# Sample attention in four 32-column groups of TensorE, old-key transposes in two parts, three unread products in the final stage

## What is computed

```python
def sample_attention(q, k_new, v_new, k_cache, v_cache, rel_bias):
    k = jnp.concatenate([k_cache, k_new], axis=1)      # 512 old rows + 16 new ones
    v = jnp.concatenate([v_cache, v_new], axis=1)
    ...
    return band_attention(q, k, v, q_pos, k_pos, k_pos >= 0, rel_bias)

def band_attention(q, k, v, q_pos, k_pos, k_valid, rel_bias):
    s = jnp.einsum('nqhd,nkhd->nhqk', q, k) * (HEAD_DIM ** -0.5)
    ...                                                # + bias by clipped distance
    p = jax.nn.softmax(s, axis=-1)
    return jnp.einsum('nhqk,nkhd->nqhd', p, v)
```

## Time and profile before

| | us |
|---|---|
| median of three runs | 1889.56 (1889.5 to 1892.87) |
| profiled execution, its own time | 1889.39 |
| profiled execution, span | 1887.7 |
| sample attention, from the first key transpose to the first product of the convolution | 455.26 to 570.61 |
| one steady turn of its loop | 13.33 |
| final stage, from the last expert's result to the end | 1830.4 to 1887.7 |

### The profile page before, as it was taken

The page is one execution under the profiler, slowest core; times in us unless marked ns, Lnnn a source line. Parts: engine busy times, 40 slices in busy tenths (PEclk is TensorE's granted clock), DMA queues, the critical chain, the costliest instruction groups (busy, mean ns, idle before and its releaser), DMA issues.

```text
span 1887.7 us, 22614 instructions
## 1 busy us (share of the span) xinstructions
PE 1708.9 (91%) x8539; PEld 1399.3 (74%) x8539; DVE 947.6 (50%) x1156; ACT 755.3 (40%) x869; POOL 261.1 (14%) x327
## 2 busy tenths in 40 slices
PE   6984999999989999999999997189999999999976
PEld 1244987887549989999999786177777777877753
DVE  0451101554321263222213544858888888888857
ACT  0221123664111112111112222157777777777753
POOL 2003501110000000000000000402121212212003
PEclk9996999999999999999999998589999999999988
DMA  9757622002512110121114433089999999999967
GB/s 343 279 99 204 207 73 73 1 1 92 160 68 79 36 45 27 51 83 52 47 51 136 181 124 134 15 330 397 400 396 400 397 399 398 398 399 397 400 223 276
DMA packets 194749, 371.36 MB, mean 197 GB/s; under 512 B 10700, under 2 KB 69108, under 8 KB 194547
## 3 DMA queue, kind: packets, MB, share of 16 engines
q1 hardware_dynamic: 170784, 289.92, 42.7%
q0 software_dynamic: 18976, 62.93, 10.4%
q10 hardware_dynamic: 4914, 17.49, 2.3%
HBM read 324.49 MB, written 47.89 MB: 197 GB/s over the span
## 4 chain that ended last, share of the span: by engine, by line
PE 72%; DMA 12%; DVE 8%; issue 3%; ACT 2%; another core or an unknown queue 2%; SPq 0%; POOL 0%; DVEq 0%; ACTq 0%; PEldq 0%; POOLq 0%
PE ps L1547 12%; PE ps L1548 12%; PE ps L1549 12%; DMA mraw<-in_w_e_down_dram 9%; PE ps L1530 4%; PE ps L1870 4%; PE ps L1871 4%; PE ps L1877 3%; PE ps L1674 3%; PE ps L1655 2%; PE ps L1897 2%; PE ps L1905 2%; PE ps L1898 2%; PE ps L1737 2%
## 5 line engine op out<-in xcount | busy, mean ns | idle before, releaser
L1064 DVE TENSOR_TENSOR mlo<-mraw,mhi 128x2048 fp32r<-128x2048 f32 x188 | 427.5, 2289 | 78.0 <-ACT mhi L931 77.8
L931 ACT CAST mhi<-mraw 128x2048 fp32r<-128x2048 f32 x192 | 366.6, 1913 | 111.5 <-DMA mraw<-in_w_e_down_dram 76.4
L1547 PE MATMUL ps<-hTh,ring_r 128*128 128x384 f32 x864 | 291.3, 337 | 38.3 <-DVE ring_r L1064 31.1
L1548 PE MATMUL ps<-hTl,ring_r 128*128 128x384 f32 x864 | 290.5, 336 | 0.0
L1549 PE MATMUL ps<-hTh,ring_r 128*128 128x384 f32 x864 | 290.2, 336 | 0.0
L1870 PE MATMUL ps<-mhi,xTh 128*128 128x512 f32 x512 | 204.6, 400 | 2.7 <-DVE xTl L1064 2.4
L1871 PE MATMUL ps<-mhi,xTl 128*128 128x512 f32 x512 | 201.5, 394 | 0.0
L1547 PEld LDWEIGHTS ps<-hTh,ring_r 128*128 128x128 f32 x864 | 163.5, 189 | 39.7 <-DVE ring_r L1064 29.3
L1064 DVE TENSOR_TENSOR ring_r<-ring_f,ring_r 128x1024 fp32r<-128x1024 f32 x56 | 68.3, 1224 | 197.8 <-ACT ring_r L741 197.4
L1548 PEld LDWEIGHTS ps<-hTl,ring_r 128*128 128x128 f32 x864 | 163.6, 189 | 0.0
L1549 PEld LDWEIGHTS ps<-hTh,ring_r 128*128 128x128 f32 x864 | 163.6, 189 | 0.0
(11 more groups left out here) (304 smaller groups left out, 2604.7 us busy)
## 6 DMA issues: line engine op xcount, KB each, us to landing
mraw<-in_w_e_gate_dram SPq DMA_DIRECT2D x64, 1024.0 KB
mraw<-in_w_e_up_dram SPq DMA_DIRECT2D x64, 1024.0 KB
mraw<-in_w_e_down_dram SPq DMA_DIRECT2D x64, 1024.0 KB, 12.6
aring<-in_w_ada_dram SPq DMA_DIRECT2D x24, 1024.0 KB
ring_f<-in_w_in_dram SPq DMA_DIRECT2D x80, 256.0 KB, 4.5
y_d<-yy ACTq DMA_DIRECT2D x32, 512.0 KB, 6.8
y_d<-zrow POOLq DMA_DIRECT2D x68, 128.0 KB, 4.1
kc<-in_cache_attn_k_dram SPq DMA_DIRECT2D x8, 1024.0 KB, 5.9
```

The costliest lines, as they stand in the source:

```text
L931: nc.scalar.copy(mhi[j][:], mraw[j][:]).then_inc(s["gu_hi" if j < 4 else "d_hi"], 1)
L1064: V.tensor_tensor(out, value, high.bitcast(F32), ALU.subtract).then_inc(sig, 1)
L1547: mm(out, xh, wh, start=start, stop=False)
L1548: mm(out, xh, wl, start=False, stop=False)
```

## The change

Scores: `qblk` now holds 32 columns for each head pair, without the zeros. Each head pair's product has a 32-column weight and writes its own 32 partitions of the bank; nothing is added up over the four. In the built program these products carry a tile of 128 rows by 32 columns at column 0, 32, 64 or 96. Values: for every head pair, a 32-column piece of `PTs` is multiplied with that pair's 128 columns of `vc`, again into its own 32 partitions, so 16 + 4 products of 128 columns take the place of 4 + 1 of 512, and the result is 128x128. `atts` becomes 128x128, its transpose one product into bank 7, and `sample_cols` two copies of 64x4x16. PE's wait for `ks_at` moves from ahead of the transposes of `Ps` to ahead of the values. The old-key transposes are cut into two halves, with the second behind the transposes of `Ps`; `k_tr` counts to two for a sequence, and ACT's copy needs only the first half. In the final stage PE waits for all 18 `wdiag` and runs three products into bank 7 that nobody reads.

```diff
-        qblk = at("qblk", [P, 2, 640], X(9))
+        qblk = at("qblk", [P, 2, HP, 32], X(9))
...
             def old_keys(q):
-                wait(sp, s["k_tr"], q - 1)
+                wait(sp, s["k_tr"], 2 * (q - 1))
...
             def old_keys_half(q):
-                act.wait_ge(s["k_tr"], q + 1)
+                act.wait_ge(s["k_tr"], 2 * q + 1)
...
             def old_keys_rest(q):
-                dve.wait_ge(s["k_tr"], q + 1)
+                dve.wait_ge(s["k_tr"], 2 * q + 2)
...
             def sample_cols(q):
                 dve.wait_ge(s["ks_att"], q + 1)
-                for h in range(H):
-                    m, rows = h // 2, slice(HD * (h % 2), HD * (h % 2) + HD)
-                    c = m * P + h * DEC
-                    V.tensor_copy(qT[rows, m, NP_TOK + q * DEC:NP_TOK + (q + 1) * DEC], ps[rows, 6, c:c + DEC]
+                cols_of = ps[:, 7, P:2 * P].rearrange("p (m h t) -> p m h t", m=HP, h=2)
+                for h_ in range(2):
+                    rows = slice(HD * h_, HD * h_ + HD)
+                    V.tensor_copy(qT[rows, :, NP_TOK + q * DEC:NP_TOK + (q + 1) * DEC], cols_of[rows, :, h_, :]
                                   ).then_inc(s["ks_at"], 1)
...
                 for m in range(HP):
-                    mm(ps[:, 4, :], qb[:, m, :], kcT[:, m, :], start=(m == 0), stop=(m == HP - 1))
+                    mm(ps[32 * m:32 * m + 32, 4, :], qblk[:, q % 2, m, :], kcT[:, m, :], start=True, stop=True)
...
                 if q + 1 < SEQS:
-                    old_keys_t(q + 1)
+                    old_keys_t(q + 1, 0)
                 pe.wait_ge(s["ks_p"], q + 1)
                 wait(pe, s["ks_ptc"], 2 * q)
-                wait(pe, s["ks_at"], H * q)
...
+                if q + 1 < SEQS:
+                    old_keys_t(q + 1, 1)
                 pe.wait_ge(s["ks_ptc"], 2 * q + 2)
                 wait(pe, s["ks_ev"], q)
+                wait(pe, s["ks_at"], 2 * q)
...
                 for c in range(4):
-                    mm(ps[:, 7, :], PTs[:, c, :], vc[:, r, c, :], start=(c == 0), stop=False)
-                mm(ps[:, 7, :], PTs[0:DEC, 4, :], v16[:, r, :], start=False, stop=True).then_inc(s["ks_pv"], 1)
+                    for m in range(HP):
+                        mm(ps[32 * m:32 * m + 32, 7, 0:P], PTs[:, c, 32 * m:32 * m + 32],
+                           vc[:, r, c, m * P:(m + 1) * P], start=(c == 0), stop=False)
+                for m in range(HP):
+                    last = mm(ps[32 * m:32 * m + 32, 7, 0:P], PTs[0:DEC, 4, 32 * m:32 * m + 32],
+                              v16[:, r, m * P:(m + 1) * P], start=False, stop=True)
...
+            pe.wait_ge(s["f_w"], 2 * NT)
+            for j in range(3):
+                mm(ps[:, 7, :], wdiag[:, 0, j, :], wdiag[:, 0, 4:8, :], start=True, stop=True)
             for t in range(NT):
-                pe.wait_ge(s["f_w"], 2 * t + 2)
```

More of the change, by code:

```diff
@@ L205, in build @@
         Ss = at("Ss", [P, NK], X(0))
-        atts = at("atts", [P, DA], X(3))
+        atts = at("atts", [P, P], X(3))
         v16 = at("v16", [DEC, 2, DA], X(5))
-        qblk = at("qblk", [P, 2, 640], X(9))
+        qblk = at("qblk", [P, 2, HP, 32], X(9))
         U = at("U", [P, HP, NP_TOK + 2], A(90))
@@ L397, in load_caches @@
                                  ).then_inc(s[f"v_in{q % 2}"], 16)
-                sp.wait_ge(s["ks_at"], H * SEQS)
+                sp.wait_ge(s["ks_at"], 2 * SEQS)
             for u, halves in enumerate(ada_units):
@@ L1143, in _ @@
             att_cols(NA // 2 - 1)
-            link(V.memset(qblk[:, :, :], 0.0))
+            link(V.memset(qblk[:], 0.0))
             dve.wait_ge(s["sb_in"], 16 * H)
@@ L1190, in _ @@
                 link.finish()
-                V.tensor_scalar(atts[:], bank(7), rinv[:, 64 + q:65 + q], None, ALU.mult
+                V.tensor_scalar(atts[:], ps[:, 7, 0:P], rinv[:, 64 + q:65 + q], None, ALU.mult
                                 ).then_inc(s["ks_ev"], 1)
@@ L1696, in _, with old_keys_t @@
             pe.wait_ge(s["s_attc"], HP * NPT)
-            def old_keys_t(q):
+            def old_keys_t(q, half):
                 r = q % 2
-                pe.wait_ge(s[f"k_in{r}"], 16 * (q // 2 + 1))
-                wait(pe, s["k_trc"], 2 * q)
-                for m in range(HP):
+                if half == 0:
+                    pe.wait_ge(s[f"k_in{r}"], 16 * (q // 2 + 1))
+                    wait(pe, s["k_trc"], 2 * q)
+                for m in (2 * half, 2 * half + 1):
                     for c in range(4):
@@ L1711, in sample_scores @@
                 wait(pe, s["ks_sb"], q)
-                qb = qblk[:, q % 2, 0:512].rearrange("p (m c) -> p m c", m=HP)
                 for m in range(HP):
-                    mm(ps[:, 4, :], qb[:, m, :], kcT[:, m, :], start=(m == 0), stop=(m == HP - 1))
+                    mm(ps[32 * m:32 * m + 32, 4, :], qblk[:, q % 2, m, :], kcT[:, m, :], start=True, stop=True)
                 for m in range(HP):
-                    last = mm(ps[:, 5, 0:DEC], qb[:, m, :], kTs[:, m, q * DEC:(q + 1) * DEC],
-                              start=(m == 0), stop=(m == HP - 1))
+                    last = mm(ps[32 * m:32 * m + 32, 5, 0:DEC], qblk[:, q % 2, m, :],
+                              kTs[:, m, q * DEC:(q + 1) * DEC], start=True, stop=True)
                 last.then_inc(s["ks_sc"], 1)
-            old_keys_t(0)
+            old_keys_t(0, 0)
+            old_keys_t(0, 1)
             sample_scores(0)
@@ L1731, in _ @@
                 tr(ps[0:DEC, 5, P:2 * P], Ps[:, PAST:NK], ident[:]).then_inc(s["ks_pt"], 1)
+                if q + 1 < SEQS:
+                    old_keys_t(q + 1, 1)
                 pe.wait_ge(s["ks_ptc"], 2 * q + 2)
                 wait(pe, s["ks_ev"], q)
+                wait(pe, s["ks_at"], 2 * q)
                 pe.wait_ge(s[f"v_in{r}"], 32 * (q // 2 + 1))
                 for c in range(4):
-                    mm(ps[:, 7, :], PTs[:, c, :], vc[:, r, c, :], start=(c == 0), stop=False)
-                mm(ps[:, 7, :], PTs[0:DEC, 4, :], v16[:, r, :], start=False, stop=True).then_inc(s["ks_pv"], 1)
+                    for m in range(HP):
[4 more added lines that the diff above has]
+                              v16[:, r, m * P:(m + 1) * P], start=False, stop=True)
+                last.then_inc(s["ks_pv"], 1)
                 if q + 1 < SEQS:
@@ L1741, in _ @@
                 pe.wait_ge(s["ks_ev"], q + 1)
[L1742 to L1745, removed]
+                tr(ps[:, 7, P:2 * P], atts[:], ident[:]).then_inc(s["ks_att"], 1)
+            pe.wait_ge(s["ks_at"], 2 * SEQS)
             project(UCC, "gev_conv", 0, True)
```

8 lines of the change are left out of this document (4 added, 4 removed).

## The result

| | before | after |
|---|---|---|
| median, us | 1889.53 (1887.86 to 1892.87, four runs) | 1829.66 (1827.22 to 1831.86, four runs) |
| ratio | | 0.968, 95% interval 0.9665 to 0.9696 |
| profiled execution: its time, its span | 1889.39, 1887.7 | 1827.22, 1825.5 |
| sample stage, first key transpose to first product of the convolution | 455.26 to 570.61: 115.35 | 455.46 to 507.99: 52.53 |
| one steady turn | 13.33 | 5.98 |

The spans differ by 62.2 us: 62.8 less in the sample stage, 1.9 more in the long middle, 1.4 less at the end, and a stage that begins 0.2 later. (The profiled execution after was the fastest of its four, so the profiles differ by 2.3 us more than the medians.)

What follows compares the result with a forecast made beforehand. The sample stage was taken as one closed loop without slack on PE. Seven turns 24.7 us less, start 1.5, last turn 4.0, final stage 0.8: 31.0 less, so 1858.5 us, range 1843 to 1885.

Steps and rivals of the forecast that it cites:

- the middle value for the overlap: Sample-stage products: only neighbouring groups overlap, values 3.25 us, scores 2.34, a turn 9.70 for 13.33; 50%, 1858.5 us.
- all four side by side: Rival for the sample-stage products: all four column groups run together, a turn 6.9 to 8.4 us, 1836 to 1848; 13%.
- the 0.07 us between two issues: Values of a sample turn: shortest spacing found, so 40 pairs of load and pass take 2.80 us, values 3.25.
- the 0.6 given back behind it: Convolution behind the sample stage: it begins at 1.2 GHz, 0.6 us lost, leaving the last turn 4.0 less.
- the last turn: Last turn of the sample stage, 14.91 us: copies, values, `atts` and transposes together 4.6 us less.
- The head of the turn: From the bias step to the first value pass: 4.11 us becomes 3.51, with 0.1 lost by the split.
- The loss by the split: Second half of the old-key transposes, ahead of the values: 0.1 us lost a turn (0 to 0.2).
- The serial rival: Sample-stage products do not overlap: a turn 12.63 us, 7.7 us less in all, 1881.9; 27%.
- Weight loads that don't hide: Rival: each of 56 passes a turn pays 0.09 us for its load, a turn 17.7 us, 1922 in all; 7%.
- The three signs that were to prove the forecast wrong: Sample stage: line 1714 starts 0.43 us apart for all eight passes, idle ahead of weight loads, clock below 1.00.
- the upper end: Unread products, final stage: if PE's clock is back by 1842, tile 0 is up to 1.87 us earlier.
- the lower end: Unread products, final stage: tile 0 begins 0.7 us later, as slowly as before; the store may land when it did.

## Why the prediction was wrong

**The bound was read rightly.** Sample attention was one closed loop on PE, and what it lost in length the end lost: 62.8 us of the stage, 62.2 of the span.

**The step that failed** is the choice of the middle value for the overlap: "the second pass of a group runs beside the first of the next, and n products take n + 1 passes". It rested on the assumption that PE starts its products strictly in program order. It doesn't: the first passes of the four groups start 6.7 ns apart, and where a second product of the same group stands between them in the program (old keys, then new keys), still 13 to 17 ns apart. The runs with 4, 6 and 8 passes in a row show how far this goes. So 2 x 0.45 and what lies around it replace five passes of 0.43: 1.00 instead of 2.34 us. The rival that had it (all four side by side, 13%) named the very condition, that the second pass of a group must be "overtaken by another group", and was put down as unlikely for want of a row; no row spoke against it either. Between two ends with no row near, the middle was taken as if it assumed the least.

**A second number failed with it**, the 0.07 us between two issues from four small transposes, which made 3.25 us of the values and put even the rival's time at 1836 and above. The values' five blocks, 40 passes, took 1.38 us, 0.035 a pass, and passes of different groups start 6.7 ns apart. The transposes load 128 columns of weights each, the values 32 (eight such loads in 0.16 us); whether that set the 0.07 no run shows. A bound was taken from an unlike row and used as a floor, which it was not.

Per turn the sizes of the miss add up: values 1.87, scores 1.34, new keys 0.46 (0.14 in the chain for 0.60), head 0.05, together 3.72 = 9.70 - 5.98. Seven turns are 26.0 of the 32.0 us by which the stage was forecast too long (62.8 measured, 30.8 forecast without the 0.6 given back behind it); the start was shorter by 3.33 instead of 1.5, the last turn by 8.7 instead of 4.6, mostly since its values took 1.48 us at full clock where 5.1 at 1.2 GHz were forecast.

**What was right.** The head of the turn: 3.51 forecast, 3.46 measured. The loss by the split: 0.1 (0 to 0.2) forecast, none measured. The copies and waits that were put at nothing cost nothing, one of them by luck: DVE's copy of the upper half of the keys was to be covered by scores that come 6.4 us behind the bias step or later. They came at 4.8, and the copy ended 0.04 us ahead of them (470.65 and 470.69). The serial rival: 1881.9 with a turn of 12.63 forecast, 1875.62 with 11.90 measured when it was built with one group; of the 0.73 between them 0.35 are the new keys and 0.28 the values. Weight loads that don't hide: excluded by the eight loads in 0.16 us, seven of which begin while passes of other groups run. By the rule of the Trainium skill ("TensorE: Matmul & The Clock Gate", Part 3) (loads overlap with running products only where the row groups differ) that rival would have held; the trace differs: all row groups are the same here, and the loads hide. The 2.38 times that the same section of the Trainium skill gives for three column tiles put the end, as an estimate, 14 us earlier than my sum, near 1844.5: on the right side of it, and still short, as 3.55 us of scores in 1.00 are 3.5 times for four tiles. The three signs that were to prove the forecast wrong (starts 0.43 us apart, idle time ahead of the weight loads, a lower clock) all looked to the slower side; the sign that came is the one given for all four side by side, a spacing under 8.5 us.

**The clock behind the stage**: 0.6 us were given back for a convolution that begins at 1.2 GHz. It does: its first 3.23 us hold 10 passes at 0.52, where in the kernel before they held 18 at 1.00, and 8 x 0.17 is 1.4 us. That is most of the 1.9 us that the middle is longer; the other 0.5 were not traced. The last turn has PE busy in 2.71 of 6.22 us, and the clock falls at its end. The window of the kernel before:

```profile
570.61:573.84 3.23, 3.23 (x18) 3.23 (x19) 0.07 (x1) 0.00 (x0) 0.51 (x1) 1.00 0.63 177
```

**The unread products**: 0.8 was forecast inside -0.7 to 1.87; between 0.4 and 1.4 came of them, by the profile that they are compared with. The clock was back by tile 0, and DVE began on it 1.35 us earlier than before and 1.9 earlier than without them, as the upper end had it; whether the store then takes some of it back, as the lower end had it, the spread of its length (6.72 to 8.27 us) hides.

## What to carry to other kernels

Where float32 products with few weight columns wait for PE, give neighbouring products different 32-column groups and alternate the groups: here four groups made them 3.5 times shorter, and up to four passes of one group in a row cost next to nothing (1.07 us for 1.03), while six or eight made the others wait. When such a stage shrinks, read next what its loads and the clock behind it do, and where a gain fails to show, follow the wait that took its place: a 3 MB broadcast store beside the weight loads cost some 30 us here.

## What the runs showed of the hardware

- Passes in different column groups start 6.7 ns apart and run side by side, all with the same 128 rows; four groups make 8 passes of 512 columns in 1.00 us instead of 3.55, and 32 of 128 columns in 1.03 instead of 3.63. Two groups make 6.96 into 3.54.
- A column group takes four passes, one that runs and three that wait: with four in a row the groups start 14 to 17 ns apart. Behind a full group nothing is handed out to the others: starts are 0.25 us apart with six passes in a row and 0.467 with eight.
- Weight loads of 32 columns begin while passes of other groups run: eight in 0.16 us.
- A store of 3068 KB out of 8 partitions took 65.7 us (48 GB/s), one of 767 KB 17.8. In 20 us beside the long one the queue of the weight loads passed 160 packets, 0.08 MB, as many packets as the store's queue; once the short one had landed, 2544 packets, 1.27 MB, in 5 us.
